# Output projection of a hybrid decoder layer: four full token tiles in two pairs, each pair by seven half-size products

## The reference

```python
merged = jax.nn.sigmoid(gate_a) * branch_a + jax.nn.sigmoid(gate_b) * branch_b
h = h + jnp.einsum('bld,de->ble', merged, w_out)      # 1024 x 1024

u = rmsnorm(h, norm_ffn)
grp_logits = jnp.einsum('bld,dg->blg', u, w_router_group) + b_router_group
exp_logits = jnp.einsum('bld,de->ble', u, w_router_expert) + b_router_expert
# top-1 group of 4, then top-2 of its 4 experts; each expert a SwiGLU of width 256
```

## Time and profile before

| | us |
|---|---|
| median of 3 runs | 889.31 (887.92 to 889.67) |
| the profiled execution, its own time | 888.84 |
| its span in the trace | 887.1 |
| what lies around the span | 1.7 |
| output projection with the router inside it | 521.7 to 596.4 |
| from its end to the first expert's transposes | 596.4 to 609.4 |

### The profile page before, as it was taken

The page is one execution under the profiler, slowest core; times in us unless marked ns, Lnnn a source line. Parts: engine busy times, 40 slices in busy tenths (PEclk is TensorE's granted clock), DMA queues, the critical chain, the costliest instruction groups (busy, mean ns, idle before and its releaser), DMA issues.

```text
span 887.1 us, 11862 instructions
## 1 busy us (share of the span) xinstructions
PE 868.0 (98%) x4657; PEld 564.0 (64%) x4657; DVE 387.2 (44%) x839; ACT 242.8 (27%) x494; POOL 153.6 (17%) x186
## 2 busy tenths in 40 slices
PE   9999999999999999999999999999999999999996
PEld 4546777888789877777777755555444444444452
DVE  3223559866546324785644552234321111103553
ACT  2201254466223210342011102120211111125554
POOL 0324311012243314200300240002000000003100
PEclk9999999999999999999999999999999999999999
DMA  9412342202020201322132235005999999785111
GB/s 362 180 82 83 133 129 91 96 1 102 1 98 3 96 1 43 160 95 95 42 149 95 95 107 229 24 29 214 405 365 365 369 370 361 293 302 176 59 51 47
DMA packets 18373, 133.03 MB, mean 150 GB/s; under 512 B 2352, under 2 KB 2864, under 8 KB 11152
## 3 DMA queue, kind: packets, MB, share of 16 engines
q1 hardware_dynamic: 12176, 103.28, 30.3%
q0 software_dynamic: 5424, 26.45, 8.6%
q10 hardware_dynamic: 720, 2.56, 0.8%
HBM read 115.47 MB, written 21.01 MB: 154 GB/s over the span
## 4 chain that ended last, share of the span: by engine, by line
PE 88%; ACT 4%; DVE 4%; issue 2%; DMA 1%; POOL 0%; POOLq 0%; DVEq 0%; ACTq 0%
PE pair L713 15%; PE single L1194 12%; PE single L892 11%; PE pair L1102 7%; PE pair L1183 6%; PE pair L788 4%; PE pair L764 3%; PE pair L1296 3%; PE pair L913 3%; PE single L913 3%; PE single L1171 2%; PE pair L1234 2%; PE single L968 1%; PE single L990 1%; PE single L987 1%
## 5 line engine op out<-in xcount | busy, mean ns | idle before, releaser
L713 PE MATMUL pair<-mem 128*128 128x288 f32 x640 | 159.4, 408 | 0.0
L713 PEld LDWEIGHTS pair<-mem 128*128 128x128 f32 x640 | 120.2, 190 | 35.9 <-ACT mem L1317 1.9
L1194 PE MATMUL single<-mem 128*128 128x512 f32 x256 | 112.8, 593 | 1.4 <-DVE mem L2140 1.4
L892 PE MATMUL single<-mem 128*128 128x288 f32 x448 | 110.2, 407 | 0.1
L892 PEld LDWEIGHTS single<-mem 128*128 128x128 f32 x448 | 84.9, 190 | 24.8 <-issue 1.1
L1194 PEld LDWEIGHTS single<-mem 128*128 128x128 f32 x256 | 47.4, 190 | 54.7 <-issue 53.1
L1317 ACT ACTIVATE mem<-single 128x256 f32<-128x256 f32 (+5 forms) x113 | 46.3, 420 | 128.0 <-PE single L1111 51.0
L1317 ACT ACTIVATE mem<-pair 128x512 f32<-128x512 f32 (+5 forms) x83 | 36.6, 492 | 153.3 <-PE pair L713 56.6
L2133 DVE SCALAR_TENSOR_TENSOR mem<-single,mem 128x256 f32<-128x256 f32 x16 | 7.7, 483 | 138.8 <-PE single L1194 126.3
L1102 PE MATMUL pair<-mem 128*128 128x512 f32 (+1 forms) x192 | 64.6, 527 | 0.5 <-DVE mem L1980 0.5
L1296 PE MATMUL pair<-mem 128*128 128x512 f32 (+1 forms) x192 | 63.4, 524 | 0.9 <-DVE mem L2186 0.9
(11 more groups left out here) (385 smaller groups left out, 1163.2 us busy)
## 6 DMA issues: line engine op xcount, KB each, us to landing
mem<-in_w_gu SPq DMA_DIRECT2D x16, 2048.0 KB, 9.2
mem<-in_w_down SPq DMA_DIRECT2D x16, 1024.0 KB, 11.7
y_slots<-mem SPq DMA_DIRECT2D x16, 512.0 KB, 3.5
y_slots<-in_zeros POOLq DMA_DIRECT2D x8, 512.0 KB, 8.3
mem<-in_w_ga SPq DMA_DIRECT2D x2, 2048.0 KB, 8.4
mem<-in_w_gb SPq DMA_DIRECT2D x2, 2048.0 KB, 8.5
mem<-in_w_wo SPq DMA_DIRECT2D x2, 2048.0 KB, 8.3
mem<-in_w_pg SPq DMA_DIRECT2D x2, 2048.0 KB, 11.1
```

Source lines behind the costliest of these rows:

```text
L713: last = nc.tensor.matmul(pb[:, hf, 0:HALF], w(k), rhs[:, k, hf * HALF:(hf + 1) * HALF], start=(k == 0), stop=(k == kk - 1))
L892: last = nc.tensor.matmul(single[plan.buf[s]][:, 0:HALF], lhs[:, k, :], rhs[:, k, :], start=(k == 0 and j in (0, 1, 3, 4)), stop=(k == 3), ...
L1194: last = nc.tensor.matmul(single[3][:, :], xT[u % 2][:, k, :], w_gu[u][:, k, :], start=(k == 0), stop=(k == KD - 1))
```

## The change

Tiles 0 and 1, and tiles 2 and 3, become pairs. In a pair the rows are split by channel halves (A0, A1 for the first tile, B0, B1 for the second; half 0 is the channel chunks 0, 1, 4, 5) and the weights by channel half and column half: Wnh, n the column half, h the channel half. Seven products `("sx", p, j)`, each of 128 tokens by 512 channels by 512 columns (four matrix products, 8 records), take the place of eight:

- j = 0: A0 by W00; j = 1: A1 by W01; j = 2: (A0 - B0) by (W11 - W10); j = 3: (B0 + B1 - A0) by (W11 - W10 + W00); j = 4: (B0 + B1) by (W10 - W00); j = 5: B1 by (W01 - W11 + W10 - W00); j = 6: (A1 + A0 - B0 - B1) by W11.

VectorE forms the four weight sums once (`sxT`, each 128 x 2048) and four sets of rows per pair (`sxS`, four operations of 128 x 512). ScalarE copies product 0 (`wpart[0]`), VectorE adds product 3 and then product 2 to it (`sxu`). GpSimd adds these parts to `h2` (`sxp`: one addition, one, and two), VectorE the rest (`wo`, one addition of 128 x 512 for each tile and column half). Products 5 and 6 accumulate onto the banks of 2 and 4. Tile 4 is computed as before, but last; `ORDER` = 1, 0, 3, 2, 4. The load of expert 1's weights now waits for `("sx", 1, 5)`, since weight sums lie in its space.

```diff
-ORDER = [0, 4, 1, 2, 3]
+ORDER = [1, 0, 3, 2, 4]
...
+    def wo_pair(p, early):
+        out = []
+        for j in range(7):
+            out += early[j] + [("sx", p, j)]
+            out += {1: [("sxp", p, 0), ("wo", 2 * p, 0)], 3: [("sxu", p), ("sxp", p, 1)] + [("sxS", 1, i) for i in range(3) if p == 0],
+                    4: [("wo", 2 * p + 1, 1), ("sxp", p, 2)], 5: [("wo", 2 * p + 1, 0)], 6: [("wo", 2 * p, 1)]}.get(j, [])
+        return out
...
-    for i, t in enumerate(ORDER):
-        s += [("wo", t, 0)]
...
-    y, z = ORDER[3:]
-    s += [("idv", t) for t in ORDER[:2]] + [("x2b", z), ("rank", y), ("rt", z), ("rtT", z), ("ids", y)]
+    s += wo_pair(0, [[("sxT", 0), ("sxS", 0, 0), ("sxT", 1), ("sxS", 0, 1), ("sxT", 2)], [], [("sxS", 0, 2)], [("sxT", 3)], [], [], []])
+    x2 = lambda t: [("x2a", t), ("sqa", t)]
+    s += wo_pair(1, [x2(1), [("x2b", 1)], [("rt", 1)] + x2(0), [("rtT", 1), ("x2b", 0)], [("rank", 1), ("rt", 0)],
+                     [("rtT", 0), ("ids", 1)], [("rank", 0)] + x2(3)])
+    s += [("x2b", 3), ("wo", 4, 0), ("ids", 0)] + x2(2) + [("rt", 3), ("x2b", 2), ("wh", 4), ("rtT", 3), ("ovp", 0), ("wo", 4, 1)]
+    s += [("rt", 2)] + x2(4) + [("rank", 3), ("rtT", 2), ("idv", 1), ("x2b", 4), ("ids", 3), ("rank", 2), ("rt", 4), ("idv", 0), ("ids", 2), ("rtT", 4)]
+    z = 4
...
+            free[1] = ("sx", 1, 5)
...
+                elif k0 == "sx":
...
+                    if j == 3:
+                        pe.wait_ge(sem("sx_p0"), p + 1)
+                    if j == 5:
+                        pe.wait_ge(sem("sx_part"), 2 * p + 2)
...
+                        pe.wait_ge(sem("sum_w"), {2: 1, 3: 3, 4: 2, 5: 4}[j])
+                    if j in (2, 3, 4, 6):
+                        pe.wait_ge(sem("sum_rows"), 3 * p + {2: 1, 3: 2, 4: 2, 6: 3}[j])
...
+                elif k0 == "sxT":
+                    i = s[1]
+                    if i == 0:
+                        mm_wait(dve, ("uy", 1, 1, 1, 6))
+                        dve.wait_ge(sem("mT"), 6)
+                        dve.wait_ge(sem("mTv"), 2)
...
+                    V.tensor_tensor(to, plus, minus, ALU.subtract).then_inc(sem("sum_w"), 1)
...
+                elif k0 == "sxu":
+                    p = s[1]
+                    mm_wait(dve, ("sx", p, 3))
+                    dve.wait_ge(sem("sx_p0"), p + 1)
...
+                    V.tensor_tensor(wpart[1], wpart[0], sx_bank[3], ALU.add).then_inc(sem("sx_part"), 1)
+                    dve.wait_ge(sem("sx_part"), 2 * p + 1)
+                    V.tensor_tensor(wpart[2], wpart[1], sx_bank[2], ALU.add).then_inc(sem("sx_part"), 1)
...
+                    if t < 4:
+                        p = t // 2
+                        j, pre = {(0, 0): (1, 1), (1, 1): (4, 2), (1, 0): (5, 4), (0, 1): (6, 4)}[(t % 2, n)]
+                        mm_wait(dve, ("sx", p, j))
+                        dve.wait_ge(sem("sx_pre"), 4 * p + pre)
+                        to = h2[:, t, n * 512:n * 512 + 512]
+                        V.tensor_tensor(to, to, sx_bank[j], ALU.add).then_inc(ev(k0), 1)
...
+                elif k0 == "sxp":
...
+                    if i == 0:
+                        pool.wait_ge(sem("sx_p0"), p + 1)
+                        add(ta, 0, wpart[0]).then_inc(sem("sx_pre"), 1)
+                    elif i == 1:
+                        pool.wait_ge(sem("sx_part"), 2 * p + 2)
+                        add(tb, 1, wpart[2]).then_inc(sem("sx_pre"), 1)
+                    else:
+                        add(tb, 0, wpart[1])
+                        add(ta, 1, wpart[1]).then_inc(sem("sx_pre"), 2)
```

More of the change, by code:

```diff
@@ L282, in __init__ @@
                     last[("single", b)] = s
-            if k in PAIR or k in SINGLE:
+            if k == "sx":
+                nmm += 1
+                self.mm[s], self.before[s] = nmm, None
+            if k == "wo" and s[1] == 4:
+                nmm += 1
+                self.mm[s] = nmm
+                self.buf[s], self.before[s] = s[2], (None, ("wo", 3, 0))[s[2]]
+                last[("pair", s[2])] = s
+            elif k != "wo" and (k in PAIR or k in SINGLE):
                 nmm += 1
@@ L452, in build @@
         h2 = view(CS, NT, D)
+        half_rows = lambda t, h: mT.rearrange("p (a h b) c -> p a h b c", a=2, h=2)[:, :, h, :, t * P:t * P + P]
+        half_w = lambda i, h: ring[(13 + i) % RING].rearrange("p (a h r) -> p a h r", a=2, h=2)[:, :, h, :]
+        sum_w = [view(at, 2, 1024) for at in (slot(0), slot(4), RINGO, slot(8))]
+        sum_rows = [[view(at + 512 * i, 2, 2, P) for i in range(4)] for at in (RINGO + 2048, SQ)]
+        wpart = [view(slot(24 + i), 512) for i in range(3)]
         pp = [view(RINGO + 7168 + D * ((t + 1) % NT), D) for t in range(NT)]
@@ L517, in build @@
         single = [ctx.enter_context(nc.psum_tensor(f"single{i}", [P, 512], F32)) for i in range(4)]
+        sx_bank = [pair[i // 2][:, i % 2, :] for i in (0, 1, 2, 0, 3, 2, 3)]
         idp = [pair[0][:, 1, 0:2 * NEXP], pair[1][:, 1, 0:8 * NEXP]]
@@ L1093, in _ @@
                     w = chunk(out).rearrange("p (k c) -> p k c", k=KD)
-                    first = s == ("wo", ORDER[0], 0)
+                    if s == ("wo", 4, 0):
+                        pe.wait_ge(sem("sx_part"), 4)
                     for i in range(4) if k0 == "wh" else range(4 * out[2], KD):
                         k = KORD[i]
[L1097 to L1100, removed]
                         for rows, cols in sides(t):
@@ L1332, in _ @@
                     copy(u2T[POS[t] % 2][:, 0:4, 0:n], single[plan.buf[s]][:, 0:4 * n].rearrange("p (k w) -> p k w", k=4)).then_inc(ev(k0), 1)
+                elif k0 == "sx" and s[2] == 0:
+                    mm_wait(act, s)
+                    if s[1]:
+                        act.wait_ge(sem("sx_pre"), 1)
+                        act.wait_ge(sem("sx_part"), 1)
+                    else:
+                        act.wait_ge(sem("mT"), 6)
+                        act.wait_ge(sem("mTv"), 2)
+                    copy(wpart[0], sx_bank[0]).then_inc(sem("sx_p0"), 1)
                 elif k0 == "sqa":
@@ L2412, in _ @@
                         pool.dma_start(iota, a["iota"]).then_inc(sem("ld_iota"), 16)
-                elif k0 == "wo" and s[2] == 1:
+                elif k0 == "sxp":
+                    _, p, i = s
+                    ta, tb = 2 * p, 2 * p + 1
+                    add = lambda t, n, part: G.tensor_tensor(h2[:, t, n * 512:n * 512 + 512], h2[:, t, n * 512:n * 512 + 512], part, ALU.add)
+                    pool.wait_ge(sem("ld_h"), 16)
+                    if i == 0:
+                        pool.wait_ge(sem("sx_p0"), p + 1)
+                        add(ta, 0, wpart[0]).then_inc(sem("sx_pre"), 1)
+                    elif i == 1:
+                        pool.wait_ge(sem("sx_part"), 2 * p + 2)
+                        add(tb, 1, wpart[2]).then_inc(sem("sx_pre"), 1)
+                    else:
+                        add(tb, 0, wpart[1])
+                        add(ta, 1, wpart[1]).then_inc(sem("sx_pre"), 2)
+                elif k0 == "wo" and s[2] == (0 if s[1] in (1, 3) else 1):
                     t, n = s[1], ntok(s[1])
```

63 lines of the change are left out of this document (49 added, 14 removed).

## The result

The changed kernel took **896.15 us** (median of 4, 895.28 to 897.48) against 889.44 for the one before (4 runs): ratio 1.0076, 95% interval [1.0058, 1.0095], 6.7 us slower. I had forecast 888.3 with a range up to 891.5.

The account below looks back on a forecast made before the run. TensorE, busy 98% of the span, was taken to bound the kernel. The projection ending 5.9 us earlier and a tail 4.9 us longer gave -1.0 us: 888.3 on the median's scale, range 886.0 to 891.5.

Parts of the forecast that it names:

- Products, -7.05: Output projection: 14 product groups instead of 16, each 3.52 us on TensorE, save 7.05 us.
- Start of the weight sums and wait before product 3: Projection's head: VectorE's weight sums start at 525.1; TensorE waits 2.3 us for product 3's weights.
- The wait before product 2: First pair in the projection: TensorE waits 0.4 us for product 2.
- before product 6: First pair: product 6 starts 1.1 us late, behind VectorE's row sums beside GpSimd's additions.
- The transposes of tile 3: Second pair: tile 3's transposes stand right behind the addition they need, costing 0.45 us.
- Small steps, -2.0 and -1.1: Projection: router pieces moved behind its end save 2.0 us; copies no longer waited for save 1.1.
- The collision with GpSimd: Projection: each GpSimd addition beside VectorE operations with both inputs in SBUF costs VectorE 1.1 us.
- End of the projection, 590.5: Last projection product ends near 590.5 instead of 596.4, 5.9 us earlier.
- "3.52" us for product 3's group: First pair: product 3's four products of 512 columns take 3.52 us.
- Tail, +4.9: After the projection: VectorE's longer queue brings the last logits 8.7 us after its end, not 3.8: 4.9 us more.
- The rest, 600.20 to the gather at 605.04, has the same steps.: Tail from the last logits on VectorE to the gather: same steps as before, no time added.
- Rival C: Wait before product 3 halves TensorE's clock for one group, 3.5 us more, 891.8 in total; chance 0.15.

Follow-up runs that it names:

- e3: Changed kernel with the unused products of both e1 and e2 added: 888.04 us, ratio 1.0001 to the kernel before.
- e1: Changed kernel with two unused products of 512 columns in front of product 3 of the first pair: 892.38 us, ratio 1.0035 to the kernel before.
- e2: Changed kernel with four unused products of 256 columns in the tail, where TensorE waits for VectorE: 888.77 us, ratio 1.0007 to the kernel before.
- the second measurement: The changed kernel itself, unedited, run again for 12 executions beside the kernel before: 891.45 us, ratio 1.0031.
- e4: Changed kernel with fewer unused products in the tail (256 columns before the last rank, three of 512 behind the table): 889.75 us, ratio 1.0008 to the kernel before.
- e7: Changed kernel with the edits of e1, e2, e5 and e6 together: 886.02 us, ratio 0.9964 to the kernel before.
- e8: Changed kernel with the 64-token tile behind product 0, tail reordered, row sums late, overflow table early, three unused tail products: 882.75 us, 0.9928 to the kernel before.
- e6: Changed kernel with pair 1's four row sums moved behind the addition that product 6 waits for: 892.82 us, ratio 1.0026 to the kernel before.
- e5: Changed kernel with the overflow table's seven VectorE operations moved from the tail into the second pair: 893.14 us, ratio 1.0033 to the kernel before.
- e11: Kernel before, without its four unused products ahead of the last rank and last table: 891.34 us, ratio 1.0024 to the kernel before.
- e10: e8 without its three unused products of 256 columns in the tail: 883.97 us, ratio 0.9945 to the kernel before.

## Why the prediction was wrong, step by step

- **Products, -7.05.** Right: 14 groups (112 records) stand where there were 16, each 3.43 to 3.70 us in the chain at full clock, except one of 3.26 whose end the chain does not hold.
- **Start of the weight sums and wait before product 3.** Predicted at 525.1 and product 3 at 535.0 after 2.3 us; measured 525.17, 534.97 and 2.0 us. The wait before product 2 was 0.8, not 0.4; before product 6 0.9, not 1.1. All three, 3.6 against 3.8: close in sum because the errors offset, which is in part luck. The transposes of tile 3 waited 0.57 us where I had 0.45.
- **Small steps, -2.0 and -1.1.** Not measured one by one. In e3, at full clock, the projection ends 6.1 us earlier than before, forecast 5.9; with the products and waits as above some 3.2 us are left for these two, against 3.1.
- **The collision with GpSimd.** Right in sum, different in form. I had charged 1.1 us to the weight sum; it took its plain 2.29, GpSimd's addition was stretched to 2.71, and the row sum behind it to 1.75. So here the one that started first kept its speed and the next paid. The Trainium skill (SBUF — State Buffer, Who interferes with whom) says that the order of issue decides which of the two is blocked; the trace agrees (2.29 us unchanged, 2.71 instead of 1.24).
- **End of the projection, 590.5.** Measured 591.8; in e3, at full clock, 590.2. **This is the first failed step**: "3.52" us for product 3's group, which took 5.38. With half clock in it, products 3 to 5 took 1.7 us longer than in e1.
- **Tail, +4.9.** At full clock (e3) the last logits come 8.9 us after the last product, forecast 8.7. In the changed kernel 9.6.
- **"The rest, 600.20 to the gather at 605.04, has the same steps."** **This is the main failed step.** The steps are the same, their speed was not: 14.9 us from the last logits to the first transposes against 9.2, since about seven of the ten unused products, the last rank and the table's products stand in a row at half clock. To the gather it is 7.5 us against 4.8. My sum ended at the gather; the six unused products behind the table, which set when the transposes start (8.00 us against 5.25), were no term of it.
- **Rival C** was the right mechanism with a wrong place and price. I let it hang on one wait longer than 1.5 us and priced one group of four products (3.5 us). It struck in two places; in the tail no wait was longer than 0.85 us. My reason against it, that single waits of 1.5 us left the clock at 1.00, did not carry over to shorter waits between small products. By the stretches the head cost 1.5 to 1.7 us (changed to e1, e2 to e3) and the tail 6.5 to 6.7 (changed to e2, e1 to e3): together 8.2, which less the 1.1 us that e3 is under the kernel before make the 7.1 us of the table. I gave it 0.15. That the second measurement's median, 891.45, lies just inside my range and near this rival's 891.8 is no support for either: it hangs on how many of its executions lost the tail's clock.

The Trainium skill (TensorE: Matmul & The Clock Gate, What's actually happening) names two levels and says that the lower one comes back when the array idles. The trace agrees on the levels (0.50 and 1.00). It doesn't show what counts as idle: behind waits of 0.85 and 0.50 us with small router products between them the clock was lost here.

## What to carry to other kernels

In this kernel a wait on TensorE was priced by its length only while the clock stayed up; where waits are added next to small products, look at the granted clock in narrow stretches, and count what stands in the queue behind them at up to double its time (5.38 us for 3.69, 8.00 for 5.25 here). The unused products kept for the clock helped only in the holes (e2); behind a hole they were a cost that grew (e4). And where a cheaper scheme needs sums first, put independent work of the same engine over them before asking what the scheme saves: with all the smaller edits in place (e7), putting the 64-token tile there moved the result from 0.9964 to 0.9928 (e8), the tail's new order in it.

## What the runs showed of the hardware

- The same 2.0 us wait before product 3 cost the clock in the profiles of the changed kernel (twice), e2 and e6, and not in e4 and e5: it is not decided by the wait's length alone.
- When it fell, it was down for about 3.4 us in the head (0.81, 0.50 and 0.83 in three stretches of 2 us) and from 596.7 to 613.8 in the tail (0.50 in every narrow cut between), though TensorE was 95% busy with small and unused products there; about the last three unused products of 512 columns were at full clock again.
- In the tail, where small router products lie between the waits, the clock fell at 596.7 behind waits of 0.85 and 0.50 us (changed kernel), at 594.6 behind one of 0.85 (e6) and at 601.8 behind one of 0.98 (e11), and stayed at 1.00 behind one of 0.85 in e10.
- A GpSimd addition of 512 columns took 1.24 us on average in e6 (three in 3.72) and 2.71 when a VectorE operation of 2048 columns with two SBUF inputs had started 0.7 us before it; VectorE's operations that read PSUM took 0.69 us beside GpSimd and alone.
